# Modulation pair 0 outside the weight ring, the context of the first attention prepared before its norm, and a fixed number of blocks split before each residual part

## The chip, the core and the metric

One Trainium2 chip, one core of it. The metric is device microseconds of one execution of the program.

## What is computed

Two blocks of two layers each run over a sequence of 512 tokens of width 1024, all in fp32. The first block has a mixer (Fourier heads and convolution heads in layer 0, pooling in layer 1) and a gated feed-forward part in each layer. The second has adaptive modulation: six vectors per layer from a condition `c`, windowed attention in layer 0 (with 256 context tokens), differential attention in layer 1, and an MLP in each.

```
def swiglu_ffn(h, w_gate, w_up, w_down):
    return (jax.nn.silu(h @ w_gate) * (h @ w_up)) @ w_down
...
    mod_x = jax.nn.silu(c) @ w_ada[i] + b_ada[i]
    mod_c = jax.nn.silu(c_ctx) @ w_ada[i] + b_ada[i]
    ...
    hx = x * (1.0 + sc1) + sh1
    hc = ctx * (1.0 + csc1) + csh1
    ax, ac = window_gqa(hx, hc, a_wq, a_wk, a_wv, a_wo, a_sink, cos, sin, need_ctx)
    x = layer_norm(alpha * x + g1 * ax, ln1_g[i], ln1_b[i])
    fx = sqrelu_mlp(x * (1.0 + sc2) + sh2, mlp_w1[i], mlp_w2[i])
    ...
    ctx = layer_norm(alpha * ctx + cg1 * ac, ln1_g[i], ln1_b[i])
```

The modulations `mod_x`, `mod_c` depend on `c` alone, so they are computed inside the feed-forward parts of the first block.

## The kernel before

**Layout.** Features lie on the 128 partitions, in eight tiles (KT = 8); the tokens are columns: T = 512 of the sequence, C = 256 of the context behind them, TT = 768 together. `X` is the residual stream. An fp32 product is made of three products of rounded parts: every activation is held as `Ahi` and `Alo` (high part and residual), every weight as `whi` and `wlo`; `product` (L669) does hi x hi, lo x hi and hi x lo. The columns T to TT of `Ahi` and `Alo` are unused until the first attention.

**The weight ring.** All weights come as a stream of blocks of 1 MB (128 x 2048 fp32), in halves. The ring has RING = 3 slots. SP loads a half into `raw` as soon as the half three blocks earlier is used (`w_used`, `freed`, L476); POOL splits it into `whi` and `wlo` (`split`, L520: the high part on line 525, the residual on line 527, which overwrites `raw`); PE waits for `w_split`. Each of SP, POOL and PE runs its own list in this fixed order. One block, the last of the mixer's output product, has a place of its own (`w9`).

**Swiglu stages (L914 on PE, 1458 on ACT, 1937 on DVE).** Stage f = 0, 1 has FF_IT = 11 steps of 256 hidden features. The order of its blocks was: two blocks of modulation weights (pair 0), gate and up of step 0, then per step gate, modulation, up, modulation, down, and at the end two modulation blocks and the last down. Modulation blocks are used as they were loaded, unsplit. For pair 0 PE runs `ada(B0 + e, e, 0, 1)` (L859, matmuls on line 867) behind the norm and before the first up-products; ACT copies the rows out (`rows`), PE selects them (`ada_select`) and DVE adds the bias (`mods`). The first up-products are `columns` (L684) over gate and up together: for each feature tile k both blocks, so both must be split from k = 0 on.

**Norms.** ACT squares a tile, PE sums over the partitions (lines 707), ACT takes the root, DVE the reciprocal (L1757), PE spreads it into PSUM (L717). Then, tile by tile: DVE scales into `tmp` (L1762, L1777), ACT makes `Ahi` (L1325, L1366), DVE the residual in `Alo` (L1753, L1784) and signals `<norm>_out`.

**First attention.** Norm n5 also modulates the context: DVE scales it (L2102) and the parts go with those of the sequence. Then DVE does `X *= ALPHA` for the context (L2107) and the scaled residual for the sequence (L2108, `n5_res`). PE makes the keys (L1032), the values (block B_KV + 1, banks 0 and 1), waits for the keys' rotation (`kvA_evac`), transposes the values (L1039), waits for the copy, and makes the queries with `dense` (L741). Rotations are ACT copies with swapped halves and three DVE instructions (`rotate`, L2112 to L2119).

**Residual parts on POOL.** Behind norms l1, l2, l3 POOL computes the next residual (`norm_residual`, L626: 8 instructions on line 635, or 633 for l2, and 8 on line 638). How many blocks it splits before each of them was rounded up to a multiple of three by `ring_end`; the order is at L642 to L664. The block numbers then were B_KV 125, B_WOA 131, B_ML0 135, B_QKV 167, B_WOB 179, B_ML1 183.

## Time and profile before

| | us |
|---|---|
| median of 3 runs | 2727.52 |
| lowest, highest | 2717.09, 2739.34 |
| the profiled execution | 2729.41 |
| its span | 2727.4 |

Over the span PE is busy 2589.6 us (95%), DVE 1486.9 (55%), ACT 649.5 (24%), POOL 1357.5 (50%). Times in the rows below are microseconds from the start of this span.

### The profile page before, as it was taken

What the parts mean: (1) busy time and instruction counts of PE and PEld (TensorE: products, weight loads), DVE (VectorE), ACT (ScalarE), POOL (GpSimd) and SP (SyncE); (2) the same over time, 40 slices, a digit from 0 to 9 for tenths busy, and PEclk for the clock granted to TensorE, in tenths of its full rate; (3) what the DMA queues carried; (4) which work ended last, traced back from release to release, by engine and by line L of the source; (5) the groups of instructions that cost most, each with busy time, mean ns of one, the idle gap of its engine ahead of it and who ended that gap; (6) DMA issues with size and microseconds to landing.
All of it is one profiled execution on the core that took longest, in us unless ns stands there. A gap on an engine that the chain in (4) does not pass through costs nothing.

```text
span 2727.4 us, 39085 instructions
## 1 busy us (share of the span) xinstructions
PE 2589.6 (95%) x14176; PEld 2101.8 (77%) x14176; DVE 1486.9 (55%) x2473; ACT 649.5 (24%) x1220; POOL 1357.5 (50%) x880
## 2 busy tenths in 40 slices
PE   7989999999999989889989999999899999899997
PEld 6668888877877868656768888888688887688886
DVE  6955666456666645445453333333586666454445
ACT  2220000031000023567131111111265553211112
POOL 6374566645665654133536444444352515776661
PEclk9999999999999999899989999999899999999998
DMA  5124444434444431000111111111111111223221
GB/s 190 55 78 139 153 155 153 154 114 146 155 152 149 154 132 62 31 1 1 39 39 62 62 62 62 62 62 63 44 47 34 44 47 38 79 94 99 95 97 54
DMA packets 67388, 235.73 MB, mean 86 GB/s; under 512 B 8144, under 2 KB 9552, under 8 KB 67152
## 3 DMA queue, kind: packets, MB, share of 16 engines
q1 hardware_dynamic: 65792, 233.64, 26.0%
q8 instruction: 63, 1.03, 0.2%
q10 hardware_dynamic: 1488, 0.69, 0.1%
q14 instruction: 45, 0.37, 0.0%
HBM read 232.21 MB, written 2.10 MB: 86 GB/s over the span
## 4 chain that ended last, share of the span: by engine, by line
PE 87%; DVE 6%; ACT 2%; issue 2%; POOL 1%; DMA 1%; SPq 0%; DVEq 0%; ACTq 0%; POOLq 0%
PE ps L674 70%; PE ps L1209 2%; PE ps L1232 2%; PE ps L829 2%; PE ps L1097 2%; PE ps L1171 2%; PE ps L1083 1%; PE ps L793 1%; PE ps L1163 1%; DVE X L1795 1%; DVE Alo L1784 1%; PE ps L717 1%; PE ps L707 1%; DVE tmp L1777 1%; DMA raw<-in_stream 1%
## 5 line engine op out<-in xcount | busy, mean ns | idle before, releaser
L525 POOL TENSOR_SCALAR whi<-raw 128x1024 fp32r<-128x1024 f32 x332 | 372.2, 1121 | 1009.2 <-DMA raw<-in_stream 1009.2
L527 POOL TENSOR_TENSOR wlo<-raw,whi 128x1024 fp32r<-128x1024 f32 x332 | 805.2, 2425 | 27.7
L674 PE MATMUL ps<-Ahi,whi 128*128 128x512 f32 (+1 forms) x2128 | 728.9, 374 | 38.6 <-DVE Alo L1784 17.6
L674 PE MATMUL ps<-Alo,whi 128*128 128x512 f32 (+1 forms) x2128 | 723.1, 371 | 0.0
L674 PE MATMUL ps<-Ahi,wlo 128*128 128x512 f32 (+1 forms) x2128 | 719.7, 369 | 0.0
L2223 DVE SCALAR_TENSOR_TENSOR X<-ps,modT,X 128x512 f32<-128x512 f32 (+1 forms) x384 | 242.2, 658 | 470.1 <-PE ps L674 469.9
L674 PEld LDWEIGHTS ps<-Ahi,whi 128*128 128x128 f32 x2128 | 375.5, 190 | 118.9 <-DVE Alo L1784 18.0
L674 PEld LDWEIGHTS ps<-Ahi,wlo 128*128 128x128 f32 x2128 | 376.4, 190 | 70.7
L674 PEld LDWEIGHTS ps<-Alo,whi 128*128 128x128 f32 x2128 | 376.7, 191 | 67.0 <-issue 0.7
L674 PE MATMUL ps<-hhi,whi 128*128 128x512 f32 x1120 | 372.2, 369 | 2.2 <-DVE X L1993 1.2
L674 PE MATMUL ps<-hlo,whi 128*128 128x512 f32 x1120 | 370.9, 368 | 0.0
L674 PE MATMUL ps<-hhi,wlo 128*128 128x512 f32 x1120 | 368.3, 366 | 0.0
L674 PEld LDWEIGHTS ps<-hhi,whi 128*128 128x128 f32 x1120 | 191.7, 188 | 43.2 <-issue 4.4
L674 PEld LDWEIGHTS ps<-hhi,wlo 128*128 128x128 f32 x1120 | 193.3, 188 | 37.4
L674 PEld LDWEIGHTS ps<-hlo,whi 128*128 128x128 f32 x1120 | 192.8, 188 | 33.6
L1325 ACT ACTIVATE hhi<-tmp 128x512 fp32r<-128x512 f32 (+1 forms) x108 | 73.7, 696 | 604.4 <-DVE tmp L2209 443.6
L1969 DVE SCALAR_TENSOR_TENSOR ps<-raw,arena,ps 128x256 f32<-128x256 f32 x432 | 173.8, 479 | 38.4 <-DMA raw<-in_stream 38.4
L1993 DVE TENSOR_TENSOR X<-ps,X 128x512 f32<-128x512 f32 x176 | 121.6, 691 | 131.9 <-PE ps L674 131.6
L1325 ACT ACTIVATE arena<-ps 128x256 f32<-128x256 f32 (+5 forms) x194 | 101.5, 543 | 244.3 <-PE ps L888 67.3
L624 POOL TENSOR_SCALAR tmp<-tmp,sm 128x256 f32<-128x256 f32 (+2 forms) x96 | 63.0, 659 | 149.9 <-DVE sm L2178 149.8
L1475 ACT ACTIVATE tmp<-ps 128x512 f32<-128x512 f32 x44 | 26.3, 598 | 420.4 <-PE ps L674 419.4
L1622 ACT ACTIVATE tmp<-ps 128x512 f32<-128x512 f32 x96 | 47.1, 526 | 294.7 <-PE ps L674 292.2
(300 smaller groups left out, 2859.4 us busy)
## 6 DMA issues: line engine op xcount, KB each, us to landing
raw<-in_stream SPq DMA_DIRECT2D x428, 512.0 KB, 3.8
X<-in_xT SPq DMA_DIRECT2D x2, 1024.0 KB, 6.4
arena<-in_dft SPq DMA_DIRECT2D x1, 2048.0 KB, 16.6
out_xT<-X SPq DMA_DIRECT2D x2, 1024.0 KB, 4.3
X<-in_ctxT SPq DMA_DIRECT2D x1, 1024.0 KB, 19.1
w<-in_stream SPq DMA_DIRECT2D x2, 512.0 KB, 4.3
vec<-in_vec SPq DMA_DIRECT2D x1, 364.5 KB, 7.5
arena<-in_fmap SPq DMA_DIRECT2D x1, 256.0 KB, 12.1
```

The source lines that it names most:

```text
L525: pool.tensor_scalar(whi[:, s, part], raw[:, s, part], 1.0, 1.0, ALU.mult, ALU.mult).then_inc(sem("w_hi"), 1)
L527: pool.tensor_tensor(wlo[:, s, part], raw[:, s, part], whi[:, s, part], ALU.subtract).then_inc(sem("w_split"), 1)
L624: pool.tensor_scalar(prob, prob, sm[:, u % 8, 2:3], 1.0, ALU.mult, ALU.mult).then_inc(sem("pA"), 1)
L674: mm = pe.matmul(dst[c], w[:, b % RING, off:off + P], rhs(k, part, c0, n), start=(k == 0 and w is whi and part == 0), stop=(k == kn - 1 an ...
L829: mm = pe.matmul(ps[:, WOUT_BANK[j], :], w[:, at:at + P], a[:, k, 0:T], start=(k == 0 and w is hi and a is Ahi), stop=(k == KT - 1 and w i ...
L1097: mm = pe.matmul(ps[DH * h:DH * h + DH, 6, 0:2 * P], vA[:, ks[t], DH * g:DH * g + DH], heads[:, h], start=(t == 0), stop=(t == len(ks) - 1 ...
L1171: mm = pe.matmul(ps[:, 6, :], vB[:, t, hh * P:(hh + 1) * P], aT[:, t, :], start=(t == 0), stop=(t == NTT - 1))
L1209: mm = pe.matmul(ps[:, 6 + t % 2, 0:256], a[:, k, t * P:(t + 1) * P], w[:, (B_QKV + 2) % RING, k * 256:(k + 1) * 256], start=(k == 0 and a ...
L1325: return act.activation(dst, src, ACT.Copy, scale=scale)
L1969: mm = dve.scalar_tensor_tensor(out=to, in0=row, scalar=c, in1=acc, op0=ALU.mult, op1=ALU.add)
L1993: dve.tensor_tensor(X[:, m, 0:T], ps[:, 4 + m % 2, :], X[:, m, 0:T], ALU.add).then_inc(sem(f"{name}_dfree"), 1)
L2223: mm = dve.scalar_tensor_tensor(out=X[:, m, c0:c0 + n], in0=ps[:, 4 + len(cols) * (m % (4 // len(cols))) + c, 0:n], scalar=mod(l, 5, m, c) ...
```

## The change

- Pair 0 of each swiglu stage is loaded past the ring, into columns T to TT of `Ahi` and `Alo` (`first_pair`), by `load_first_pair`: for f = 0 behind the ring loads of the mixer, for f = 1 behind the pool block. PE uses it with `ada_first`. FF_BLOCKS falls from 57 to 55, and all later blocks have other places in the ring (B_KV 121, B_WOA 127, B_ML0 131, B_QKV 163, B_WOB 175, B_ML1 179). The stream in memory is the same; loads add `skipped`.
- Where two blocks are used together, POOL splits them in turns, half by half (`split_pair`): the first two blocks of all, gate and up of step 0, and the first two of B_WOA. `columns` waits accordingly.
- Context: ACT makes the modulated context (`context`, in the place of `Alo`), its high part and `X *= ALPHA` for it, behind its last swiglu step and before n5; DVE one residual. n5's loops cover the sequence alone. POOL splits B_KV, then waits for `n5_out` KT - 2 (six tiles), then goes on. The spread of n5 goes to bank 1, the values to banks 2 and 3; the first query block's two tiles are made by `query_tile` between the values, the transposes and the rest.
- Before each residual part POOL splits up to and with the third block of the next stage, without rounding.

The diff, cut to its core (renumbered block offsets on ACT and DVE are left out):

```diff
 SQUARES = {"n1": 6, "n2": 6, "n4": 0, "n5": 0, "l1": 0, "l2": 0, "l3": 2, "l4": 2}
-RSTD = {"n1": 7, "n2": 5, "n4": 5, "n5": 3, "l1": 4, "l2": 6, "l3": 4, "l4": 3}
-PASSES = {"l1": [(0, 1)], "l2": [(0,), (1,)], "l3": [(0,)], "n5": [(0, 1)]}
+RSTD = {"n1": 7, "n2": 5, "n4": 5, "n5": 1, "l1": 4, "l2": 6, "l3": 4, "l4": 3}
+PASSES = {"l1": [(0, 1)], "l2": [(0,), (1,)], "l3": [(0,)], "n5": [(0,)]}
...
 B_WOUT = B_WIN + 6
-FF_BLOCKS = 5 * FF_IT + 2
+FF_BLOCKS = 5 * FF_IT
 B_FF = [B_WOUT + 4, B_WOUT + 4 + FF_BLOCKS + 1]
...
 B_ML1 = B_WOB + 4
-N_BLOCKS = B_ML1 + ML_BLOCKS
+RING_BLOCKS = B_ML1 + ML_BLOCKS
+N_BLOCKS = RING_BLOCKS + 4
 B_ML = [B_ML0, B_ML1]
...
         if 0 <= at < FF_BLOCKS:
-            if at < 4:
-                return at < 2
+            if at < 2:
+                return False
             if at >= FF_BLOCKS - 3:
                 return at < FF_BLOCKS - 1
-            return (at - 4) % 5 in (1, 3)
+            return (at - 2) % 5 in (1, 3)
     return False
 SPLITS = [0]
-for _b in range(N_BLOCKS):
+for _b in range(RING_BLOCKS):
     SPLITS.append(SPLITS[-1] + (0 if is_ada(_b) else 2))
...
         Alo = sb("Alo", [P, KT, TT], F32R)
+        Alo_at = nc.sbuf_base - 4 * KT * TT
+        context = nc.alloc_sbuf_tensor_at("context", [P, KT, TT], F32, offset=Alo_at)
+        first_pair = [nc.alloc_sbuf_tensor_at(f"pair{e}", [P, KT, TT], F32, offset=at)[:, :, T:TT]
+                      for e, at in enumerate((Ahi_at, Alo_at))]
...
                     load(b, b % RING, half)
+            def load_first_pair(f):
+                if f:
+                    sp.wait_ge(*when("pair_used", 2))
+                for e in range(2):
+                    sp.dma_start(first_pair[e], ins["stream"][B_FF[f] + 2 * f + e].rearrange("p (k c) -> p k c", k=KT)).then_inc(sem(f"pair{e}"), 16)
+            load_first_pair(0)
             sp.wait_ge(*when("y_done", HEADS_A))
...
-            def load_run(first, end):
+            def load_run(first, end, skipped):
                 for b in range(first, end):
...
                         freed(b, half)
-                        load(b, b % RING, half)
+                        load(b + skipped, b % RING, half)
...
                 B0 = B_FF[f]
+                S = B0 + 2 * f + 4
+                load_run(B0, B0 + 2, 2 * f + 2)
                 with sp.Fori(0, FF_IT // 3) as p:
-                    for b in range(B0 + 4, B0 + 19):
-                        at = (b - B0 - 4) // 5 * 5 + B0 + 4 + FF_ORDER[(b - B0 - 4) % 5]
+                    for n in range(15):
+                        at = n // 5 * 5 + S + FF_ORDER[n % 5]
                         for half in range(2):
-                            freed(b, half, 5 * p)
-                            load(15 * p + at, b % RING, half)
-                for b in range(B0 + 49, B0 + 54):
+                            freed(B0 + 2 + n, half, 5 * p)
+                            load(15 * p + at, (B0 + 2 + n) % RING, half)
+                for n in range(45, 53):
+                    at = S + (45 + FF_ORDER[n - 45] if n < 50 else n)
                     for half in range(2):
-                        freed(b, half)
-                        load(B0 + 49 + FF_ORDER[b - B0 - 49], b % RING, half)
-            load_run(last + 1, B_FF[0] + 4)
+                        freed(B0 + 2 + n, half)
+                        load(at, (B0 + 2 + n) % RING, half)
+            assert last + 1 == B_FF[0]
             load_swiglu(0)
-            load_run(B_FF[0] + 54, B_FF[1] + 4)
+            load_run(B_POOL, B_POOL + 1, 2)
+            load_first_pair(1)
             load_swiglu(1)
-            first, rounds = -(-(B_FF[1] + 54) // RING), N_BLOCKS // RING
-            load_run(B_FF[1] + 54, first * RING)
+            first, rounds = -(-B_KV // RING), RING_BLOCKS // RING
+            load_run(B_KV, first * RING, 4)
             with sp.Fori(first, rounds) as i:
...
                         freed(s, half, i)
-                        load(RING * i + s, s, half)
-            load_run(rounds * RING, N_BLOCKS)
+                        load(RING * i + (s + 4), s, half)
+            load_run(rounds * RING, RING_BLOCKS, 4)
...
                     split(b % RING, half, 16 * rounds + (16 * (b // RING) + 16), more + (SPLITS[b] + half + 1))
+            def split_pair(b):
+                for half in range(2):
+                    for n in range(2):
+                        split((b + n) % RING, half, 16 * ((b + n) // RING) + 16, SPLITS[b] + 2 * half + n + 1)
...
                 B0 = B_FF[f]
-                for b in (B0 + 2, B0 + 3):
-                    split_block(b)
+                split_pair(B0)
                 with pool.Fori(0, FF_IT // 3) as p:
...
                         for b in (0, 2, 4):
-                            split_block(B0 + 4 + 5 * s + b, FF_SPLITS * p, 5 * p)
+                            split_block(B0 + 2 + 5 * s + b, FF_SPLITS * p, 5 * p)
                 for i in range(FF_IT // 3 * 3, FF_IT - 1):
                     for b in (0, 2, 4):
-                        split_block(B0 + 4 + 5 * i + b)
+                        split_block(B0 + 2 + 5 * i + b)
                 split_block(B0 + FF_BLOCKS - 1)
...
-            split_run(0, B_WOUT + 3)
+            split_pair(B_WIN)
+            split_run(2, B_WOUT + 3)
             for half in range(2):
...
             split_swiglu(1)
-            split_run(B_KV, ring_end(B_WOA))
+            split_block(B_KV)
+            pool.wait_ge(*when("n5_out", KT - 2))
+            split_run(B_KV + 1, B_WOA)
+            split_pair(B_WOA)
             for u in range(N_UNITS):
...
-            split_run(ring_end(B_WOA), ring_end(B_ML0 + 2))
+            split_run(B_WOA + 2, B_ML0 + 3)
             norm_residual("l1", 1, X_CTX)
-            split_run(ring_end(B_ML0 + 2), ring_end(B_QKV + 2))
+            split_run(B_ML0 + 3, B_QKV + 3)
             norm_residual("l2", 2, X_ONLY)
-            split_run(ring_end(B_QKV + 2), B_QKV + 11)
+            split_run(B_QKV + 3, B_QKV + 11)
             for h in range(EARLY):
...
                     split_run(B_QKV + 11, B_WOB)
-            split_run(B_WOB, ring_end(B_ML1 + 2))
+            split_run(B_WOB, B_ML1 + 3)
             norm_residual("l3", 3, X_ONLY)
-            split_run(ring_end(B_ML1 + 2), N_BLOCKS)
+            split_run(B_ML1 + 3, RING_BLOCKS)
...
                         if k % 4 == 0:
-                            pe.wait_ge(*when("w_split", ws + (k // 4 + 1)))
+                            pe.wait_ge(*when("w_split", ws + (k // 4 + 1 if len(blocks) == 1 else k // 2 - n + 1)))
                         for j in range(2):
...
-            def dense(name, b0, cols, ready, first_two=True):
+            def dense(name, b0, cols, ready, first=0):
...
                 blocks = [(SPLITS[b0 + i], b0 + i) for i in range(4)]
-                for i in ((0, 2, 3) if ready else range(4)):
+                for i in ((0, 2, 3) if ready else range(first, 4)):
                     both = bool(ready) and i == 0
...
+            def ada_first(f, e):
+                pe.wait_ge(*when(f"pair{e}", 16 * f + 16))
+                for k in range(KT):
+                    g = k % 4
+                    mm = pe.matmul(ps[ADA_GROUP * g:ADA_GROUP * (g + 1), 6 + e, 0:256],
+                                   csil[:, k, 2 * (ADA_SHARED - 1):2 * (ADA_SHARED - 1) + ADA_GROUP], first_pair[e][:, k, :],
+                                   start=(k < 4), stop=(k >= 4), skip_group_check=True)
+                mm.then_inc(sem("pair_used"), 1)
             def ada_select(name, copies):
...
                 for e in range(2):
-                    ada(B0 + e, e, 0, 1)
-                columns(f"{name}_up", [(SPLITS[b], b) for b in (B0 + 2, B0 + 3)], X_ONLY, banks[0:4], ready)
+                    ada_first(f, e)
+                columns(f"{name}_up", [(SPLITS[b], b) for b in (B0, B0 + 1)], X_ONLY, banks[0:4], ready)
                 ada_select(name, 2)
...
                     for s in range(3):
-                        i, at = 3 * p + s, B0 + 4 + 5 * s
+                        i, at = 3 * p + s, B0 + 2 + 5 * s
                         for part in range(2):
...
+            pe.wait_ge(*when("context_out", 1))
             columns("kvA_done", [(SPLITS[B_KV], B_KV)], X_CTX, [[ps[:, 4, :], ps[:, 5, 0:C]], [ps[:, 6, :], ps[:, 7, 0:C]]], "n5_out")
...
             for k in range(KT):
-                mm = product([ps[:, 0, :], ps[:, 1, 0:C]], X_CTX, B_KV + 1, k * 256, a_rhs, k, KT)
+                mm = product([ps[:, 2, :], ps[:, 3, 0:C]], X_CTX, B_KV + 1, k * 256, a_rhs, k, KT)
             mm.then_inc(sem("w_used"), 2)
+            def query_tile(j):
+                for k in range(KT):
+                    if j == 0 and k % 4 == 0:
+                        pe.wait_ge(*when("w_split", SPLITS[B_WQA] + k // 4 + 1))
+                    mm = product([ps[:, 2 * j, :], ps[:, 2 * j + 1, 0:C]], X_CTX, B_WQA, k * 256 + j * P, a_rhs, k, KT)
+                    if j == 1 and k % 4 == 3:
+                        mm.then_inc(sem("w_used"), 1)
+                if j == 0:
+                    mm.then_inc(sem("qA_done"), 1)
+            pe.wait_ge(*when("n5_res", KT))
+            query_tile(0)
             pe.wait_ge(*when("kvA_evac", 3))
...
             mm.then_inc(sem("vA_done"), 1)
+            query_tile(1)
             pe.wait_ge(*when("vA", 1))
-            dense("qA", B_WQA, X_CTX, None)
+            dense("qA", B_WQA, X_CTX, None, 1)
...
-                def rows(b_a, gap):
+                def rows(b_a):
                     for e in range(2):
-                        act.wait_ge(*block_used(b_a + gap * e))
+                        if b_a is None:
+                            act.wait_ge(*when("pair_used", 2 * f + e + 1))
+                        else:
+                            act.wait_ge(*block_used(b_a + e))
                         copy(arow[:, e, :], ps[:, 6 + e, 0:256]).then_inc(sem(f"{name}_arow"), 1)
...
                         if j:
-                            act.wait_ge(*block_used(b + 2 if first else b))
+                            act.wait_ge(*block_used(b))
                         else:
...
             swiglu(1, "ff1")
+            act.wait_ge(*when("tables", 16 * 4))
+            act.wait_ge(*when("mods", 12))
+            for k in range(KT):
+                act.activation(context[:, k, T:TT], X[:, k, T:TT], ACT.Identity, scale=s1[:, 0, k, 1:2],
+                               bias=s2[:, 0, k, 1:2]).then_inc(sem("context"), 1)
+            act.wait_ge(*when("context", KT))
+            copy(Ahi[:, :, T:TT], context[:, :, T:TT]).then_inc(sem("context_hi"), 1)
+            copy(X[:, :, T:TT], X[:, :, T:TT], ALPHA).then_inc(sem("context_res"), 1)
             rms("n5", "ff1_dfree", 8 * FF_IT, split=False)
-            split_hi_modulated("n5", 0, X_CTX)
+            split_hi_modulated("n5", 0, X_ONLY)
...
             act.wait_ge(*block_used(B_KV + 1))
-            copy(vT[:, 0:T], ps[:, 0, :])
-            copy(vT[:, T:TT], ps[:, 1, 0:C]).then_inc(sem("kvA_evac"), 1)
+            copy(vT[:, 0:T], ps[:, 2, :])
+            copy(vT[:, T:TT], ps[:, 3, 0:C]).then_inc(sem("kvA_evac"), 1)
             def take_keys(g):
...
             dve.wait_ge(*when("tables", 16 * 4))
+            dve.wait_ge(*when("context_hi", 1))
+            dve.tensor_tensor(Alo[:, :, T:TT], context[:, :, T:TT], Ahi[:, :, T:TT], ALU.subtract).then_inc(sem("context_out"), 1)
             norm_rstd("n5", T)
...
                     modulated("n5", 0, k, 0, 0, 0, T)
-                    dve.tensor_scalar(tmp[:, k % 4, T:TT], X[:, k, T:TT], s1[:, 0, k, 1:2], None, ALU.mult).then_inc(sem("n5_m"), 1)
                 if k >= 1:
-                    split_lo_modulated("n5", 0, k - 1, 0, X_CTX)
-            dve.wait_ge(*when("n5_m", 2 * KT))
+                    split_lo_modulated("n5", 0, k - 1, 0, X_ONLY)
+            dve.wait_ge(*when("n5_m", KT))
             for k in range(KT):
-                dve.tensor_scalar(X[:, k, T:TT], X[:, k, T:TT], ALPHA, None, ALU.mult)
                 dve.scalar_tensor_tensor(out=X[:, k, 0:T], in0=X[:, k, 0:T], scalar=rg[:, 0, k:k + 1], in1=norm_scale("n5", 0, T),
...
             dve.wait_ge(*when("n5_res", KT))
+            dve.wait_ge(*when("context_res", 1))
             for j in range(8):
...
                     dve.wait_ge(*block_used(B_WOA + j // 2))
```

## Rows read from the trace of the kernel before

**Rows 1.** The page, part 4: the chain that ended last, share by engine.
```profile
PE 87%; DVE 6%; ACT 2%; issue 2%; POOL 1%; DMA 1%; SPq 0%; DVEq 0%; ACTq 0%; POOLq 0%
```
**Rows 2.** PE's waits: waiting line, releaser, us in total, times, longest.
```profile
PE ps L674 <- POOL wlo L527: 11.8, 3, 6.2
```
**Rows 3.** PE in time: start, duration (us), instruction, idle before and its releaser.
```profile
22.80 0.79 PE L674 MATMUL ps<-Ahi,whi 128*128 128x512 f32 x1 [0.74 <-POOL wlo L527]
...
189.24 0.50 PE L674 MATMUL ps<-Ahi,whi 128*128 128x512 f32 x1 [0.20 <-DVE Alo L1753]
...
613.08 0.50 PE L674 MATMUL ps<-Ahi,whi 128*128 128x512 f32 x1
...
1016.72 1.01 PE L674 MATMUL ps<-Ahi,whi 128*128 128x512 f32 x2 [6.82 <-DVE Alo L1784]
...
1046.21 0.87 PE L1039 MATMUL ps<-ident,tmp 128*128 128x128 f32 x6 [2.10 <-DVE arena L2119]
1048.14 0.62 PE L674 MATMUL ps<-Ahi,whi 128*128 128x512 f32 x2 [1.05 <-DVE arena L2129]
...
1312.00 1.01 PE L674 MATMUL ps<-Ahi,whi 128*128 128x512 f32 x2 [3.25 <-DVE Alo L1753]
```
**Rows 4.** Stretches: bounds, length, busy time per engine, granted clock, DMA share, GB/s.
```profile
197.00:203.00 6.00, 5.91 (x15) 4.69 (x16) 6.00 (x6) 3.12 (x5) 5.83 (x5) 0.56 0.10 8
203.00:221.00 18.00, 18.00 (x85) 15.03 (x84) 1.65 (x3) 1.94 (x5) 5.95 (x3) 1.00 0.13 42
1014.00:1022.00 8.00, 5.28 (x18) 4.51 (x19) 8.00 (x10) 2.06 (x4) 4.81 (x3) 0.53 0.00 0
1047.00:1054.00 7.00, 5.95 (x25) 5.01 (x25) 0.96 (x1) 0.00 (x0) 5.40 (x4) 0.76 0.24 92
```
**Rows 5.** The chain in order of time: start, duration, what.
```profile
197.09 23.11 PE ps L674 x90
221.00 11.04 PE ps L674 x48
...
619.58 23.46 PE ps L674 x90
```
**Rows 6.** SP's queue and POOL in time; the page's issues (KB, us to landing).
```profile
174.36 6.24 SPq L451 DMA_DIRECT2D raw<-in_stream  x6
...
185.14 1.05 POOL L525 TENSOR_SCALAR whi<-raw 128x1024 fp32r<-128x1024 f32 x1 [17.57 <-DMA raw<-in_stream]
...
raw<-in_stream SPq DMA_DIRECT2D x428, 512.0 KB, 3.8
...
arena<-in_dft SPq DMA_DIRECT2D x1, 2048.0 KB, 16.6
...
X<-in_ctxT SPq DMA_DIRECT2D x1, 1024.0 KB, 19.1
```
**Rows 7.** DVE in time, norm n5, beside POOL (1012.81) and with POOL idle (1024.90).
```profile
1009.94 0.75 DVE L1777 SCALAR_TENSOR_TENSOR tmp<-X,s,ps 128x512 f32<-128x512 f32 x1 [1.25 <-PE ps L717]
...
1012.81 3.86 DVE L1784 SCALAR_TENSOR_TENSOR Alo<-tmp,s,Ahi 128x512 fp32r<-128x512 f32 x2
...
1024.90 1.13 DVE L1784 SCALAR_TENSOR_TENSOR Alo<-tmp,s,Ahi 128x512 fp32r<-128x512 f32 x2
```
**Rows 8.** ACT and DVE in time: end of swiglu, norm n5, and 768 columns.
```profile
991.54 0.38 ACT L1325 ACTIVATE arena<-ps 128x256 f32<-128x256 f32 x1 [0.48 <-PE ps L867]
...
1007.74 0.95 DVE L1757 RECIPROCAL std<-std 128x128 f32<-128x128 f32 x1 [2.96 <-ACT std L1341]
...
1071.50 0.85 ACT L1325 ACTIVATE std_r<-arena 128x768 fp32r<-128x768 f32 x1
...
1075.54 0.94 DVE L2132 TENSOR_TENSOR rstd_r<-arena,std_r 128x768 fp32r<-128x768 f32 x1
```
**Rows 9.** POOL's residual part l2 and DVE's query rotation beside POOL.
```profile
1993.46 2.30 DVE L2116 TENSOR_TENSOR tmp<-tmp,arena 128x512 f32<-128x512 f32 x1
...
1999.11 11.03 POOL L633 TENSOR_TENSOR X<-X 128x512 f32<-128x512 f32 x8
```

More of the change, by code:

```diff
@@ L199, in build @@
         shared["oB_early"] = ("bands", 46)
+        shared.update(pair0=("x0", 16), pair1=("x1", 16), pair_used=("sig", 4))
+        shared.update(context=("csilu", 4), context_hi=("csm", 2), context_res=("pf", 4), context_out=("u", 4))
         share("y", {n: KT for n in norms if n not in ("n3", "n5")})
@@ L202, in build @@
             share(signal, {n: 2 * KT if n == "l2" else KT for n in norms if n != "l4"})
-        share("m", {"n5": 2 * KT, "l1": 2 * KT, "l2": 2 * KT, "l3": KT})
+        share("m", {"n5": KT, "l1": 2 * KT, "l2": 2 * KT, "l3": KT})
         share("mu", {n: 1 for n in norms[5:]})
@@ L943, in swiglu @@
                 i = FF_IT - 2
-                at = B0 + 4 + 5 * i
+                at = B0 + 2 + 5 * i
                 for part in range(2):
@@ L951, in swiglu @@
                 i = FF_IT - 1
-                b = B0 + 4 + 5 * i
+                b = B0 + 2 + 5 * i
                 for e in range(2):
@@ L1481, in step @@
                         copy(hhi[:, slot, j, 0:T], tmp[:, j, 0:T]).then_inc(sem(f"{name}_hi"), 1)
-                rows(B0, 1)
+                rows(None)
                 step(0, B0, 0, True)
@@ L1486, in swiglu @@
                     for s in range(3):
-                        step(3 * p + s + 1, 15 * p + (B0 + 4 + 5 * s), (s + 1) % 3, False, s == ADA_SHARED - 1)
-                step(FF_IT - 1, B0 + 4 + 5 * (FF_IT - 2), (FF_IT - 1) % 3, False)
-                rows(B0 + 4 + 5 * (FF_IT - 1), 1)
+                        step(3 * p + s + 1, 15 * p + (B0 + 2 + 5 * s), (s + 1) % 3, False, s == ADA_SHARED - 1)
+                step(FF_IT - 1, B0 + 2 + 5 * (FF_IT - 2), (FF_IT - 1) % 3, False)
+                rows(B0 + 2 + 5 * (FF_IT - 1))
             rms("n2", "wout_evac", 0)
@@ L2008, in swiglu @@
                 for j in range(2):
-                    hidden(0, B0 + 3, j, True)
+                    hidden(0, B0 + 1, j, True)
                 mods(0, 0, 1)
@@ L2015, in swiglu @@
                         for e in range(2):
-                            ada_sums(p, 3 * p + s, e, B0 + 5 + 5 * s + 2 * e, s or e)
+                            ada_sums(p, 3 * p + s, e, B0 + 3 + 5 * s + 2 * e, s or e)
                         if s == ADA_SHARED - 1:
                             dve.wait_ge(*when(f"{name}_acc", ADA_SUMS * ADA_SHARED * (p + 1)))
-                        step(3 * p + s, 15 * p + (B0 + 4 + 5 * s), (s + 1) % 3, p if s == ADA_SHARED - 1 else None)
-                step(FF_IT - 2, B0 + 4 + 5 * (FF_IT - 2), (FF_IT - 1) % 3, last=True)
+                        step(3 * p + s, 15 * p + (B0 + 2 + 5 * s), (s + 1) % 3, p if s == ADA_SHARED - 1 else None)
+                step(FF_IT - 2, B0 + 2 + 5 * (FF_IT - 2), (FF_IT - 1) % 3, last=True)
                 mods(4, 10, 2)
```

## The prediction

> **What bounds the kernel now.** I read the page's chain first: 87% of the chain that ended last is PE [rows 1]. So a change gains only where PE stands still or runs slowly, and what it moves on DVE, ACT, POOL or a queue is free as long as PE doesn't wait for it. PE's own list of waits comes second: POOL's weight splits stop it in three places only, 11.8 us in all [rows 2]. PE in order of time gives the places [rows 3]: 0.74 us before 22.80 (the first product), 6.82 us before 1016.72 (the key product of the first attention), 2.10 and 1.05 us around the transposes at 1046.21. The other two waits for POOL, 6.2 us the longer, come after the first gate tiles of the two swiglu stages, at 189.24 and 613.08, and end at 197.09 and 619.58, where the chain goes on [rows 3, 5]. The table of stretches adds what follows a wait: 0.56 of the clock granted from 197 to 203, 1.00 from 203, so most of those six microseconds ran at the lower level, 1.2 GHz, and the rest at 2.4 [rows 4]. A pause is paid twice, idle and slow. At full clock the pace is 48 matmuls of 512 columns in 11.04 us [rows 5].
>
> **The start (first two blocks split in pairs).** PE stops before the second block, whose first half was split third. It is now split second, one half (about 4 us) earlier, so the 0.74 us go: 0.7. Bounds 0 (DVE's tiles are the limit then) and 1.5 (some slow pace goes as well).
>
> **The two swiglu starts (pair 0 past the ring).** Before, the pair takes the first two ring places, so the second up-block is loaded only after PE has used the pair, behind the norm. PE's passes over the pair stay as they are, and the first gate product stays at 189.24 and 613.08, because its activations decide that. What goes is the wait for the second block. In layer 0 gate and up now take the places that the pair had, whose loads start at 174.36 and some 2.7 us later; a load lands in 3.8 us, and POOL, idle 17.57 us before 185.14, can begin near 178.2 [rows 6]. Four halves of about 3.5 us end near 192.8. From 189.24 all 96 matmuls run on: 96/48 x 11.04 = 22.1 us, to 211.3. Before, the last 90 ended at 197.09 + 23.11 = 220.2: gain 8.9. In layer 1: 613.08 + 22.1 = 635.2 against 619.58 + 23.46 = 643.0: gain 7.8 [rows 3, 5]. The activations keep up: PE wants a tile each 2.8 us, and even beside POOL two residuals of DVE took 3.86 us [rows 7]. Bounds: 0.3 more or 2 less in each stage, by where POOL's instruction stands when the first residual is due.
>
> What is moved: four DMAs of 1 MB in pieces of 1 KB, ahead of others on SP's queue. The first two are issued near 90 us, behind the ring loads of the input product; next on the queue are loads that wait some 30 us for the transforms anyway. The other two stand behind the pool block, near 565, ahead of gate and up of layer 1. Price by rows: the context's load (pieces of the same size) landed 19.1 us after its issue, the transform matrix ahead of it, issued half a microsecond earlier, 16.6 [rows 6]; so 1 MB of them costs about 3 us, the two 6, and by the raw 19.1 each, 38. Gate and up aren't wanted before 613: loaded by 580 (or 603 in the worst case, plus their own 4 and 14 us of splits: up to 8 us too late). I take 0, with the small price.
>
> POOL's four halves for layer 1 then fall into 579 to 594, beside DVE's last residuals of the pool stage. Such an instruction (two SBUF inputs) took 1.93 us beside POOL and 0.57 in the mean alone [rows 7]. One or two are met, and PE works meanwhile on earlier groups: I take 0, bounds 0 and 3 us of loss.
>
> **The attention start (context ahead, POOL held back).** ACT is free from 991.92 until the down-products end near 1004. It gets eight instructions of 256 columns (0.38 each, 3.0 in all), a copy and a scaling of 2048 columns (from 0.38 for 256 and 0.85 for 768: 2.0 each), then its table load (1.28) and the first four squares (2.2): done near 1002.5 [rows 8]. DVE, free at 1004.78 (the reciprocal at 1007.74 had waited 2.96), gets one subtraction of 2048 columns: by 0.94 for 768 it takes 2.5 and ends at 1007.3, ahead of the reciprocal [rows 8]. Both are covered, by 1.5 and 0.4 us; uncovered they would cost 7.0 and 2.5. DVE's loop loses eight scalings and eight residual parts of the context and, behind it, eight scalings by ALPHA. More counts that POOL stops after B_KV (near 1004.6) until the sixth tile is out: two residuals took 3.86 us beside it, 1.13 without [rows 7]. DVE starts at 1009.94; scaling 0.75, ACT's copy and a residual of about 0.7 each with the handovers make 2.4 us: PE starts at 1012.3 instead of 1016.72, 4.4 gained. Behind POOL's new wait stands B_KV+1: sixth tile near 1018.7, split by 1026, wanted at 1031; then B_WQA by 1033, wanted at 1039. Both in time.
>
> The values go to other banks and the first query tile (some 8.5 us) fills the time in which the keys are rotated. The waits of 2.10 and 1.05 go, 3.2, and with them the slow pace behind: 0.76 of the clock over 7 us, 1.7 [rows 3, 4]. The slow pace at the key product was 2.4 us (0.53 granted in the stretch, PE slow from 1016.72 to some 1021.5). After a pause of 2.4 us instead of 6.8 I take 1.8 of it as left, so 0.6 gained: after the pauses of 3.2 us around 1046 it was 1.7, and here PE was lightly loaded before. Bounds 0 and 2.4. Together 4.4 + 3.2 + 1.7 + 0.6 = 9.9, bounds 7.5 and 12. The rest of the queries is the same work, and the idle behind it (the last tiles' rotation) stays.
>
> The Trainium skill (TensorE: Matmul & The Clock Gate, section on the HAM clock gate) says that the throttled state is the default and that activity lifts it. By it the restart at 1012.3 pays its full 2.4 again and the stage gives 9.3. The row at 1016.72 agrees; for a pause as short as 2.4 us none decides.
>
> **Fixed number of blocks ahead.** Before l1 and l3 it is three blocks before and after (ring_end gave 138 for 137 and 186 for 185). Before l2 it is three in place of four: POOL's residual part starts near 1988 instead of 1999.11, and 7 us of splits move behind it. Beside it DVE rotates the queries, on which the first scores hang. A rotation part met by a split took 2.30 us [rows 9]; an instruction of the residual part is 11.03/8 = 1.4 us, so three of DVE's parts may lose up to 1.4 each, and the later split 2 less or more. I take 0, bounds -3 and +4. B_WOA's second block is split earlier, but PE's start at 1312.00 waited for DVE's residual, not for POOL [rows 3]: 0.
>
> The Trainium skill (SBUF — State Buffer, "Who interferes with whom") has a DVE instruction with two SBUF inputs and a GpSimd instruction that reads SBUF shut each other out for a whole instruction. By it l2 would lose 4 us; that is rival (b). The pair of 3.86 us agrees with it.
>
> **Sum.** 0.7 + 8.9 + 7.8 + 9.9 = 27.3 us off the profiled execution's own 2729.4 us (span 2727.4; 1.9 above the median of 2727.5): 2702.1.
>
> **Rivals.** (a) The clock falls inside the up phases although PE doesn't pause. For it: PE did little for 10 us before. Against: no stretch shows it without a pause. It keeps 2.4 and 2.8 us (23.11 and 23.46 less 20.7 for 90 matmuls): 2707. (b) The shared port: 3 us at the pool stage and 4 at l2: 2709. Against: PE has earlier work in both places. (c) The change doesn't do what it says at the attention: ACT's added work delays the squares, or B_KV+1 comes late, and 6 to 10 of the 9.9 go: 2708 to 2712. (d) The other side: every later block has another ring place, and in each step of the loops a load or a split comes just too late. There are 20 + 30 steps; from 27.3/50 = 0.55 us in each the kernel is slower, and at 1 us it is 2752. Against: order and distance of the loads in a step are unchanged, and PE waited for POOL three times in all. (e) More than summed: full clock at 1012.3 and less contention at the first diff-attention units, 4 to 5 us: 2697.
>
> **How the numbers follow.** Forecast 0.60 (its own range 2698 to 2706), (a) 0.12, (b) 0.08, (c) 0.05, (d) 0.03, (e) 0.12. About 1% (27.3 us) is what a measurement of this kernel can tell from no change, and the sum lies on it: half of 0.60 and (e) make faster 0.42, the other half with (a), (b) and (c) same 0.55, (d) slower 0.03. The range runs from 2692 (e with the other upper bounds) to 2715 (c and part of b).
>
> **What would show it.** Right: no wait for POOL after the first gate tile; an up phase of 22 us from there; keys 2.4 us behind DVE's first scaled tile; the end of the query products 10 us nearer to that tile. Wrong: a granted clock under 0.9 inside an up phase; PE waiting for POOL at B_KV+1; n5's reciprocal late; a new wait in the steps of the loops, repeated 50 times.

## Result and profile after

The changed kernel takes 2701.28 us in the median of 4 runs (2693.92 to 2704.22), the kernel before 2727.4: a ratio of 0.9899 with an interval of 0.9853 to 0.9945. So it is about 1% faster, and the interval excludes 1. The forecast was 2702.1. The two profiled executions differ by more, 2729.41 against 2693.92 us, so the spans were taken apart between instructions that both kernels have. Each kernel was traced a second time, unchanged (before_again and after_again, below), to see what repeats. The first four marks are the first spread matmuls of norms n2, n4, n5 and the end of the last query product of the first attention; the next are the first woA product, the last spread group of l1, the first of l2, and the first scores of the differential attention. Each entry is a difference of two starts or ends in the trace, in us.

| stretch | before, two traces | changed, two traces | gain of the means | forecast |
|---|---|---|---|---|
| start to n2 | 184.39, 182.28 | 181.84, 181.63 | 1.6 | 0.7 |
| n2 to n4 (layer 0) | 424.25, 424.00 | 417.68, 417.31 | 6.6 | 8.9 |
| n4 to n5 (layer 1) | 400.10, 400.47 | 392.63, 391.24 | 8.4 | 7.8 |
| n5 to end of queries | 109.03, 109.11 | 99.70, 98.56 | 9.9 | 9.9 |
| window attention, to woA | 194.23, 194.29 | 191.77, 197.13 | -0.2 | 0 |
| woA and norm l1 | 84.43, 85.88 | 85.90, 85.86 | -0.7 | 0 |
| MLP of layer 0, to l2 | 557.72, 558.30 | 548.78, 558.84 | 4.2 | 0 |
| l2 to first scores | 58.21, 56.76 | 57.52, 56.35 | 0.6 | 0 |
| rest | 715.04, 714.21 | 716.28, 714.88 | -1.0 | 0 |

The first four rows hold the forecast sum: 26.5 us against 27.3. The other 9 us between the first two traces lie in one row, the MLP of layer 0, and the same kernel gave both values. Each stage was also left as it is in the changed kernel by most of the experiments below. Over all traces that leave it so (11, 8, 11 and 9 of them), the four gains are 1.8, 8.1, 8.0 and 10.0, 27.9 us together.

PE in order of time at the places of [rows 3], changed kernel, first trace (start, duration, instruction, idle before and releaser):
```profile
19.52 0.79 PE L705 MATMUL ps<-Ahi,whi 128*128 128x512 f32 x1 [4.05 <-DVE Alo L1820]
...
182.92 1.93 PE L909 MATMUL ps<-pair,arena 128*32 128x256 f32 x32
187.36 0.80 PE L705 MATMUL ps<-Ahi,whi 128*128 128x512 f32 x1 [2.51 <-DVE Alo L1820]
...
996.02 0.98 PE L705 MATMUL ps<-Ahi,whi 128*128 128x512 f32 x2 [2.43 <-issue]
...
1031.79 0.71 PE L1095 MATMUL ps<-ident,tmp 128*128 128x128 f32 x5
1032.26 0.60 PE L705 MATMUL ps<-Ahi,whi 128*128 128x512 f32 x2
```
The chain in order of time, same trace, for [rows 5]:
```profile
187.36 23.66 PE ps L705 x96
...
604.17 21.98 PE ps L705 x96
```
The waits for weight splits are gone, and so are those around the transposes at 1031.79. Both up phases now run as one piece of 96 matmuls; the first takes 1.7 us more than the second. There is one wait that wasn't there: 2.51 us before the first gate product at 187.36, where [rows 3] had 0.20. PE's pass over the pair just ahead of it (L909) takes 1.93 us. In the kernel before it took 3.34:
```profile
185.70 3.34 PE L867 MATMUL ps<-raw,arena 128*32 128x256 f32 x32
```

What ACT and DVE do ahead of the attention, answering [rows 8], first trace (start, duration, instruction; ACT, then DVE, then POOL):
```profile
975.30 4.04 ACT L1577 ACTIVATE context<-X,s 128x256 f32<-128x256 f32 x8
979.37 1.92 ACT L1381 ACTIVATE Ahi<-context 128x2048 fp32r<-128x2048 f32 x1
981.20 1.90 ACT L1381 ACTIVATE X<-X 128x2048 f32<-128x2048 f32 x1
...
988.16 2.28 DVE L2166 TENSOR_TENSOR Alo<-context,Ahi 128x2048 fp32r<-128x2048 f32 x1
991.14 0.95 DVE L1824 RECIPROCAL std<-std 128x128 f32<-128x128 f32 x1 [0.70 <-ACT std L1397]
...
1002.74 1.05 POOL L547 TENSOR_SCALAR whi<-raw 128x1024 fp32r<-128x1024 f32 x1 [14.99 <-DVE Alo L1851]
```
The work moved forward is hidden as forecast: 7.9 us on ACT (7.0 forecast), and DVE's one residual ends at 990.44, before the reciprocal, which still waits for ACT. POOL stands until 1002.74.

### The profile page after: what moved, and what is told of

Read it like the earlier page. It is cut to its first block, busy times and chain, and to the rows that moved or that the text cites. A ratio compares the mean times of both kernels' runs of the same rounds, so it can differ in the third digit from the quotient of the medians.

```text
span 2692.1 us, 38964 instructions
## 1 busy us (share of the span) xinstructions
PE 2570.3 (95%) x14176; PEld 2092.8 (78%) x14176; DVE 1472.7 (55%) x2450; ACT 653.7 (24%) x1222; POOL 1356.8 (50%) x880
## 4 chain that ended last, share of the span: by engine, by line
PE 90%; DVE 6%; ACT 2%; issue 2%; DMA 0%; POOL 0%; DVEq 0%; SPq 0%; ACTq 0%
PE ps L705 71%; PE ps L1265 2%; PE ps L1288 2%; PE ps L860 2%; PE ps L1227 2%; PE ps L1153 2%; PE ps L1139 1%; PE ps L824 1%; PE ps L738 1%; PE ps L748 1%; PE ps L1219 1%; DVE X L1862 1%; PE ps L1114 1%; DVE q L2343 1%; PE ps L1113 1%
## 5 line engine op out<-in xcount | busy, mean ns | idle before, releaser
L549 POOL TENSOR_TENSOR wlo<-raw,whi 128x1024 fp32r<-128x1024 f32 x332 | 804.8, 2424 | 27.7
```

The costliest lines, as they stand in the source:

```text
L549: pool.tensor_tensor(wlo[:, s, part], raw[:, s, part], whi[:, s, part], ALU.subtract).then_inc(sem("w_split"), 1)
```

## Experiments

Times are medians; the changed kernel's, over its two series, is 2700.7 to 2701.3. A ratio is to the kernel before, run in the same series, with its interval behind it. Lengths are those of the table above.

**The changed kernel again.**

> The changed kernel once more, unchanged. The profiled executions differ by 35.3 us, the medians by 26 us; 9.0 of the 35.3 us lie in the MLP of layer 0, where the pairs of matmuls of 512 and 256 columns came every 0.353 us before and every 0.347 us after, both at a granted clock of 1.00. Theory A (my own): the pace of these pairs is a state of one execution and no effect of the change; then it may come out as 0.353 here, and single times of one kernel lie some 9 us apart. Rival B: the change brought it (other ring places); then it is 0.347 again.

2700.71 us (ratio 0.9901, 0.9872 to 0.9929). The MLP of layer 0 was the long one this time. Stretches inside it (bounds, length, PE, PEld, DVE, ACT, POOL busy, granted clock, DMA share, GB/s), first trace of the changed kernel:
```profile
1540.00:1580.00 40.00, 40.00 (x233) 34.98 (x232) 12.70 (x20) 3.52 (x7) 17.84 (x10) 1.00 0.20 66
```
and the second, after_again:
```profile
1540.00:1580.00 40.00, 40.00 (x228) 34.71 (x227) 13.61 (x22) 3.44 (x6) 18.07 (x10) 1.00 0.17 55
```
Same instructions, granted clock 1.00 in both, PE never idle: 233 matmuls in 40 us or 228. A pair of 512 and 256 columns comes every 0.347 us in one, every 0.353 in the other. The pace changes only where PE stops (for under 0.2 us in two traces, for 1 us or more in the others): in the first trace it went from 0.353 to 0.347 at the 1.04 us wait at 1397.54. In the second it is 0.353 on both sides of the same wait, and in six other traces it went the other way there. Theory A holds: 10 us in this stage that belong to the execution, not to the change. This traced execution took 2703.63 us, the first 2693.92; the window attention was 5.4 us longer in the second as well, and small differences in the other stages took as much back. Of eleven traces with such pairs in this stage, two had the short one, the first of the changed kernel and context_back.

**The kernel before again.**

> The kernel before once more, unchanged, for a second trace of it. Theory A: the pace of the 512+256 pairs in the MLP of layer 0 is a state of the execution; it may be 0.353 us again or 0.347, and the stages that the change touches keep their lengths: first gate tile to the end of the first up phase 31.0 and 30.0 us (layer 0, layer 1), 109 us from the norm's spread to the end of the query products, each within 1.5 us. Rival B: these lengths scatter by more than that; then the parts of the gain can't be read from one pair of traces.

The stages that the change touches repeat within 0.4 us, but for the start: the input product took 70.39 us in one trace and 67.90 in the other, with the same 0.74 us wait in both. Theory A, except there. The pace in the MLP was 0.353 in both.

**The second block late.**

```diff
-                load_run(B0, B0 + 2, 2 * f + 2)
+                load_run(B0, B0 + 1, 2 * f + 2)
+                sp.wait_ge(*when("pair_used", 2 * f + 1))
+                load_run(B0 + 1, B0 + 2, 2 * f + 2)
```

> SP loads the second block (up) of each swiglu stage only when PE has used the first modulation block, as the ring forced it before. Theory A (the gain of the two starts comes from that load): PE stops again after the first gate tiles, for 2.5 to 5 us each, and then runs at the lower clock for some 3 us; 3 to 6 us lost in layer 0, 4 to 6.5 in layer 1, 7 to 12 in all. Rival B (PE is held by DVE's residuals anyway): under 2 us in each.

2713.67 us (0.9948, 0.9929 to 0.9968): 12.4 to 13 us of the 26 gone. PE in time, and the chain in order of time, this run:
```profile
184.61 0.50 PE L707 MATMUL ps<-Ahi,whi 128*128 128x512 f32 x1 [0.36 <-DVE Alo L1822]
...
191.22 0.79 PE L707 MATMUL ps<-Ahi,whi 128*128 128x512 f32 x1 [4.96 <-POOL wlo L551]
```
```profile
191.22 23.22 PE ps L707 x90
...
614.52 23.23 PE ps L707 x90
```
The pattern of before is back: six matmuls, a pause, and 90 that take 23.2 us where 20.7 would do. From the first gate tile to the end of the phase it is 29.8 and 30.5 us against 22.05, so 7.8 and 8.4 lost in the phases (22.05 is the shortest first phase of any trace; the changed kernel's own two had 23.66 and 23.67). Over the whole stages it is 421.50 and 400.77 us, 4.0 and 8.8 more than the two traces of the changed kernel: in range for layer 0, where PE starts earlier behind the norm here, and above it for layer 1. Theory A: the late load of one block had cost all of the gain in layer 1, and in layer 0 4.0 of the 6.6.

**POOL not held back in norm n5.** One line out of POOL's list: `pool.wait_ge(*when("n5_out", KT - 2))`.

> POOL no longer waits for six tiles of norm n5 before it goes on to split. Theory A (POOL's splits stretch DVE's residuals, 3.86 us for two beside it, 1.13 without): the first key product starts 1 to 3 us later than in the changed kernel (3.87 us behind the spread there) and runs slowly for longer; 1.5 to 4 us in all. Rival B (the earlier context work gave the whole 4.2 us): no more than 0.5 us later. Other side: with the splits earlier, something behind gains what the start loses.

2703.4 us (0.9923, 0.9897 to 0.9948), so the total alone can't tell it from the changed kernel. The first key product starts 5.24 us behind the spread, against 3.87 and 3.59; n5 to the end of the queries takes 101.69, 2.6 more. DVE in this run:
```profile
992.73 1.56 DVE L1850 SCALAR_TENSOR_TENSOR Alo<-tmp,s,Ahi 128x512 fp32r<-128x512 f32 x1
...
996.32 2.20 DVE L1850 SCALAR_TENSOR_TENSOR Alo<-tmp,s,Ahi 128x512 fp32r<-128x512 f32 x1
```
In the changed kernel each of the first six takes 0.75. Theory A.

**First query block behind the transposes.**

```diff
-            pe.wait_ge(*when("n5_res", KT))
-            query_tile(0)
             pe.wait_ge(*when("kvA_evac", 3))
...
+            pe.wait_ge(*when("vA", 1))
+            pe.wait_ge(*when("n5_res", KT))
+            query_tile(0)
             query_tile(1)
-            pe.wait_ge(*when("vA", 1))
```

> Both tiles of the first query block come behind the transposes of the values again, as before the change; all else as changed. Theory A: the waits around the transposes (2.10 and 1.05 us before) and the slow pace behind them (1.7) are back: 4.9 us lost, the key product starts as in the changed kernel. Rival B: with POOL held back and the context's rotation earlier the keys are ready in time anyway: under 1.5 us lost.

n5 to the end of the queries takes 103.72 us, 4.6 more than the mean of the two traces of the changed kernel; the first key product starts 4.06 behind the spread as expected. PE waits again:
```profile
1022.74 0.88 PE L1093 MATMUL ps<-ident,tmp 128*128 128x128 f32 x6 [0.96 <-ACT tmp L1381]
1024.67 0.61 PE L705 MATMUL ps<-Ahi,whi 128*128 128x512 f32 x2 [1.05 <-DVE arena L2196]
```
The second wait is the old one; the first is 0.96 us, not 2.10, and ends with ACT's copy of the values. The granted clock is 0.50 from 1026 to 1028 and 1.00 from 1030. Theory A in the loss, then, with a shorter first wait, though the median of the whole kernel, 2700.64 (0.9906, 0.9881 to 0.9931), does not show these 4.6 us: with four runs and a pace that moves single times by 9, it can't.

**The context in the loop again.** ACT's block is taken out, n5's loops cover the context, DVE scales it there, and `X *= ALPHA` stands ahead of each scaled residual:

```diff
+                dve.tensor_scalar(X[:, k, T:TT], X[:, k, T:TT], ALPHA, None, ALU.mult)
                 dve.scalar_tensor_tensor(out=X[:, k, 0:T], in0=X[:, k, 0:T], scalar=rg[:, 0, k:k + 1], ...
```

> The context is modulated and scaled in the loop of norm n5 again (eight more scalings and residual parts on DVE, ACT's early block gone); POOL's wait and the order of the query tiles stay. With the run in which POOL's wait alone was taken away (key product 5.24 us behind the spread in place of 3.87, 2.0 us lost by the end of the query products) it splits the 4.2 us of the earlier start. Theory A (both count): the first key product starts 1.0 to 2.0 us later behind the spread than in the changed kernel, and 1 to 4 us are lost by the end of the query products. Rival B (POOL's wait gave it all): under 0.5 us. Other side: DVE's longer loop ends so late that the first query tile, which waits for all eight residuals of X, comes late; then over 4 us.

2710.32 us (0.9938, 0.9918 to 0.9958), 9.3 lost; n5 to the end of the queries takes 108.79, as long as before the change. The first key product is only 0.8 to 1.1 us later (4.70 behind the spread). That start scatters, too: over the ten traces in which neither POOL's wait nor the context was touched it lies 3.58 to 4.41 behind the spread, so the context's own share in the earlier start is small, below theory A's range. The rest is the other side of the expectation (DVE, one instruction of POOL, PE):
```profile
1011.87 2.48 DVE L2167 TENSOR_SCALAR X<-X 128x256 f32<-128x256 f32 x1
1014.26 0.73 DVE L2168 SCALAR_TENSOR_TENSOR X<-X,rg,ps 128x512 f32<-128x512 f32 x1
1014.92 0.48 DVE L2167 TENSOR_SCALAR X<-X 128x256 f32<-128x256 f32 x1
1015.33 0.73 DVE L2168 SCALAR_TENSOR_TENSOR X<-X,rg,ps 128x512 f32<-128x512 f32 x1
1015.98 1.91 DVE L2167 TENSOR_SCALAR X<-X 128x256 f32<-128x256 f32 x1
...
1011.76 2.44 POOL L549 TENSOR_TENSOR wlo<-raw,whi 128x1024 fp32r<-128x1024 f32 x1
...
1026.50 1.01 PE L705 MATMUL ps<-Ahi,whi 128*128 128x512 f32 x2 [3.64 <-DVE X L2168]
```
DVE ends the scaled residuals at 1026.4 and the first query tile waits 3.64 us for the last of them, then runs slowly. POOL, held for six tiles and then let go, splits beside just these instructions. The scalings of the context have one input and still took 1.9 to 2.5 us beside POOL's two-input residual (L549), 0.48 beside its one-input high part and 0.28 while POOL stood. So the order of the queries pays only with the context out of DVE's loop: undone one at a time, the three edits of this stage cost 2.6, 4.6 and 9.7 us, together more than the 9.9 that all three gain.

**The start in sequence.** `split_pair(B_WIN)` undone, with the old condition in the input product.

> The first two blocks of all are split one after the other again; all else as changed. The first trace showed the input product 2.9 us shorter than before (70.4 to 67.5) where 0.7 was forecast. Theory A (the pause of 0.74 us also kept the clock low for longer): PE stops for 0.7 us before the second block and its slow matmuls last longer; the product is 1.5 to 3 us longer than in the changed kernel. Rival B (only the wait itself counts, the rest is scatter of the clock): 0.5 to 1.0 us longer, and traces of the changed kernel differ in this stage by 1 us or more.

2708.5 us (0.9915, 0.9887 to 0.9943), 7 to 8 us above the changed kernel, of which this stage explains the smaller part; the rest is not explained (five executions, from 2694.4 to 2711.81, and a window attention of 197.31 us, at the long end, in the traced one). The input product took 69.70 us with a wait of 0.74 again, 2.3 to 2.5 more than in the changed kernel. With the two traces of before, three in sequence give 67.90 to 70.39, mean 69.3; eleven in pairs give 67.00 to 68.32, mean 67.4. So 1.9 on average, of which 0.74 is the wait. How much slow pace comes with it differs from one execution to the next; neither theory alone.

**Four blocks ahead of l2.** The residual part behind one block more.

> POOL splits four blocks, not three, before the residual part of l2, as before the change. The first traces have 45.2 us from the spread of l2 to the first scores before and 44.5 after. Theory A (the residual part's place makes nothing that can be measured): 44.3 to 45.4 us here. Rival B (the later split beside DVE's query rotation costs): over 46 us. Totals the same within 3 us of the changed kernel.

2704.23 us (0.9898, 0.9859 to 0.9937), and 45.18 us from the last spread group of l2 to the first scores, where before had 45.17 and 44.05 and the changed kernel 44.48 and 43.34. Theory A: about 1 us, below what a total can show.

**POOL held at the first swiglu start.** The new wait came from the 2.51 us at 187.36. DVE in the changed kernel, first trace:
```profile
184.47 2.83 DVE L1820 TENSOR_TENSOR Alo<-tmp,Ahi 128x512 fp32r<-128x512 f32 x1
```

```diff
-            def split_pair(b):
+            def split_pair(b, held=None):
...
                 for half in range(2):
+                    if half and held:
+                        pool.wait_ge(*when(*held))
...
-                split_pair(B0)
+                split_pair(B0, None if f else ("n2_out", 2))
```

> In the first swiglu stage POOL waits for two residual tiles of norm n2 before it splits the second halves of gate and up. In the changed kernel DVE's first residual took 2.83 us beside POOL, PE stood 2.51 us and ran slowly for 3.2. Theory A (POOL held DVE up): the residual takes 0.7 us, PE starts 1.5 to 2.2 us nearer to the norm's spread, and the up phase takes 22.1 to 22.5 us in place of 23.7: 2.5 to 4 us gained in the stage. Rival B (the clock falls anyway, since PE does little in the norm): 1.5 to 2.2 us gained. Other side: the second halves come too late (they must be split by 11 us after PE's start); then PE waits for POOL and the gain is lost.

2698.02 us (0.9879, 0.9846 to 0.9913). DVE and PE in this run:
```profile
184.21 0.69 DVE L1822 TENSOR_TENSOR Alo<-tmp,Ahi 128x512 fp32r<-128x512 f32 x1
...
184.96 0.50 PE L707 MATMUL ps<-Ahi,whi 128*128 128x512 f32 x1 [0.36 <-DVE Alo L1822]
```
PE starts 3.39 us behind the spread of n2 in all three traces with this wait, and the phase takes 22.05 to 22.06. Without the wait nine traces gave 3.39 to 3.43 four times, with a first residual of 0.69 to 0.74, and 5.15 to 5.68 five times, with one of 1.59 to 2.87: it depends on where POOL's instruction stands when that residual is due. Leaving out up_late, the whole stage took 414.0 to 415.4 us in the three with the wait, 413.9 to 415.6 in the three that were lucky without it, and 415.7 to 417.7 in the five that were not. So theory A, worth about 2 us in half of the executions, and 1.6 more where the clock falls too. That last part is not tied to the pause: l2_four paused 2.54 us in the same place and restarted at full clock. The stretch from 188 to 190, changed kernel, first trace:
```profile
188.00:190.00 2.00, 2.00 (x6) 1.63 (x5) 2.00 (x3) 1.19 (x2) 1.92 (x2) 0.50 0.03 8
```
and l2_four:
```profile
188.00:190.00 2.00, 2.00 (x11) 1.64 (x10) 2.00 (x3) 0.81 (x2) 2.00 (x1) 1.00 0.00 0
```

**Even pairs in the MLP of layer 0.** `EVEN = [(0, TT // 2), (TT // 2, TT // 2)]`, 384 and 384 columns, in place of 512 and 256. In this first form the down parts of columns 384 to 511 get the context's gate, so this part of the result is changed; the time is that of the even sizes.

> In the MLP of layer 0 the 768 columns go as 384 and 384 instead of 512 and 256, on PE, ACT and DVE. Theory A (the pace of 0.353 us for a pair comes from a small matmul beside a large one, where the weight load of the next doesn't always hide): an even pair takes 0.347 in every execution, by 832 cycles of 2.4 GHz, and the stage 538 us in place of 538 or 547; 0 to 9 us gained. Rival B (the state is not one of the sizes): pairs of 0.353 again. Rival C (a load shown with 0.19 us does not fit under 384 columns, 0.16): over 0.36 us for a pair, 20 us lost or more.

2695.29 us (0.9881, 0.9862 to 0.9901), and the stage 548.51 us. The expectations give it as 538 or 547, counted from its first to its last product; counted so it took 537.78 here, 538.05 and 548.11 in the two traces of the changed kernel. The number is theory A's; its reason, a weight load that doesn't always hide, is not shown. Its matmuls in the stretch 1450 to 1850, first of six groups alike (busy, mean ns):
```profile
L706 PE MATMUL ps<-hlo,whi 128*128 128x384 f32 x386 | 98.0, 334 | 0.0
```

**Both, complete.** DVE adds the down parts in pieces of 384, 128 and 256 columns, each with its own gate.

> Two edits on the changed kernel: POOL waits for two residual tiles of n2 before the second halves of the first gate and up (as hold_ff0), and the MLP of layer 0 goes in 384 and 384 columns on PE and ACT, while DVE adds the down parts in three pieces (384, 128 and 256 columns) since sequence and context have gates of their own. Theory A: the pair of 384 holds 0.347 us in each execution (538 us for the stage) and DVE, which has half of PE's time free there, hides a third piece of some 0.25 us for each of 256 tiles; median 2688 to 2695, 6 to 12 us below the changed kernel's 2701. Rival B (DVE's add is on the path, through the down banks that it frees): the stage is longer than 545 us.

> The kernel of both edits (POOL held for two residual tiles of n2, 384 and 384 columns in the MLP of layer 0) once more, for a third trace of the even pairs and more times. So far 0.347 us for a pair came in 2 of 2 traces with even pairs, and in 2 of 11 with pairs of 512 and 256. Theory A (the even sizes set the pace): 0.347 again, 549 us from the spread of l1 to the norm of l2; median 2690 to 2697. Rival B (those two were luck): 0.353, 558 us, median near 2698 to 2701.

2694.47 us (0.9864, 0.9837 to 0.9891), and in a second series 2690.57 (0.9848, 0.9824 to 0.9873). The stage took 549.14 us in the first trace. Three of three traces with even pairs had the pace of 0.347, against two of eleven without (548.72 us for the stage in the third). Three traces against two in eleven make luck unlikely, no more. All ten times lie at 2687.7 to 2697.27, with a mean of 2692.3, against 2699.8 for eight of the changed kernel, in other series: some 7 us below it. This is the fastest version by its medians; its ratios barely part from those of the changed kernel.

## Why the prediction was right

**Sum and median.** 27.3 forecast; 26.1 between the medians, 26.5 in the four stretches that it named. That it came within a microsecond is in part luck: 0.9 more at the start, 2.3 less in layer 0 and 0.6 more in layer 1 cancel. The profiled executions alone (35.5 apart) would have looked like rival (e). They aren't: 8.9 us are the pace of the MLP in one execution, and the window attention, which the change doesn't touch, moved by 5 between two traces of the same kernel.

**The start.** Mis-sized: 0.7 forecast with a bound of 1.5. The whole stretch gained 1.6; the input product alone 1.9 over fourteen traces, 2.9 between the first two. The wait was right; the slow pace behind it was taken as zero. What the forecast says of a pause everywhere else (idle and slow) it did not apply to the smallest one.

**Swiglu, layer 0.** 8.9 forecast, 6.6 measured in the two traces (0.6 by a later start of PE and 1.6 by slow pace behind it), 8.1 over eight. The step that failed is "the first gate product stays at 189.24, because its activations decide that". Relative to the norm they came later: 4.85 and 4.58 us behind the spread before, 5.52 and 5.15 after. POOL's 2.35 us instruction stands across DVE's first residual, which takes 2.83 us; it is 0.69 where POOL is held. POOL met that residual before the change, too:
```profile
187.25 1.94 DVE L1753 TENSOR_TENSOR Alo<-tmp,Ahi 128x512 fp32r<-128x512 f32 x1
```
It cost PE only 0.20 us then, because its pass over the pair lasted until 189.04. The forecast held "0.3 more or 2 less in each stage, by where POOL's instruction stands" as a bound; a stretched residual is that case, met in five of nine traces; with the slow pace behind it the two traces fell 2.3 short, just past the bound. "PE's passes over the pair stay as they are" failed with it: 1.93 us at a granted clock of 1.00 (182 to 184) instead of 3.34 with 0.50 granted from 186 to 188, too short to cover the residual. Why the clock fell at that pass in both traces of before and in neither of these is open.

The Trainium skill (SBUF — State Buffer, "Who interferes with whom") has this as an exclusive lock of whole instructions between DVE and GpSimd. The trace agrees for two inputs (2.83 against 0.69), and for the one-input scalings too (2.48 against 0.28), which the page allows for a `tensor_scalar` in its two-port mode.

**Rival (a)** was right in layer 0 of both traces of the changed kernel (23.66 and 23.67 us, 0.50 of the clock from 188 to 190), but after a pause, not without one as it said. In layer 1, with no pause, it was wrong: 22.05 and 22.10, and the phase of 96 matmuls at 22.1 was the forecast to the tenth.

**Swiglu, layer 1.** 7.8 forecast, 8.4 measured. The splits that moved beside DVE's last residuals of the pool stage cost nothing, though they stretched more of them than the one or two forecast: the last three took 6.53 us, where they had taken 2.15. PE did not wait for them. Its waits there are the old ones: 1.16 us at 567.23 and 1.95 at 587.04, against 1.16 at 576.38 and 1.95 at 596.18 before.

**The attention.** 9.9 forecast, 9.9 measured. The start came 4.1 and 4.3 us earlier behind the spread (4.4 forecast); the two waits at the transposes are gone, and their slow pace. The 0.6 for a shorter slow pace at the key product can't be told from the 0 of the alternative beside it (9.3 for the stage): PE's first 60 matmuls from there took 12.67 and 12.84 us before, 12.34 and 13.02 after, and 11.85 to 13.23 in the ten traces of its variants. Early work on ACT was 0.9 us longer than forecast and stayed hidden. The loads of the pairs landed in 8.2 to 11.8 us and stopped nobody.

**l2, l1, l3.** 0 forecast; 0.6, within scatter. Rival (b) is wrong there: DVE's rotation parts beside the residual part took 1.32 and 1.65 us, where one beside a split had taken 2.30 [rows 9]. Rival (d) as well: no PE wait for a split is left in either trace.

**What the forecast lacked** was not a price but the size of the noise in one trace. It made its sum against one execution and compared it with a median; that this worked owes something to the first trace of before having, as nine of eleven have, the slower pace.

## What to carry to other kernels

A wait of PE for a late weight block is paid as idle time and again as slow matmuls behind it; loading the block outside the ring removes both, but the splitting that moves forward then meets the vector engine in the norm, so hold it until the first tiles are out. Work taken out of a loop is worth most where something new is waiting for the end of that loop. Before the difference of two traces is explained, trace each kernel twice and compare stage by stage: stages that the change doesn't touch give the scatter.

## What was not expected of the hardware

- Streams of 512- and 256-column matmuls in turns run at one of two paces, 0.347 or 0.353 us for a pair, at a granted clock of 1.00 and without idle time; the pace is taken at a pause and kept to the next, for some 500 us in this stage. Pairs of 384 and 384 ran at 0.347 in all three traces. Which pace is taken, and why, stays open.
- A pause at the same instruction was followed by half the clock for some 3 us in two executions (2.51 and 2.13 us long) and by the full clock in a third (2.54).
- A one-input DVE scaling of 128x256 took 0.28 us with POOL idle, 0.48 beside POOL's one-input instruction, and 1.9 to 2.5 beside its two-input one.
